# Modulation products of a hybrid transformer block on four groups of 32 array columns

## What is computed

```python
silu_c = jax.nn.silu(c)
silu_cc = jax.nn.silu(c_ctx)
mod_l = (silu_c @ w_mod[l] + b_mod[l])[:, None, :]
mod_c = silu_cc @ w_mod[l] + b_mod[l]
sh1, sc1, gt1, sh2, sc2, gt2 = jnp.split(mod_l, 6, axis=-1)
csh1, csc1, cgt1, csh2, csc2, cgt2 = jnp.split(mod_c, 6, axis=-1)
pl = modulate(rms_norm(xl, g_mix[l]), sh1, sc1) @ w_in[l]
pc = modulate(rms_norm(xc, g_mix[l]), csh1, csc1) @ w_in[l]
...
filt_l = hyena_filter(S, hy_f_w1[l], hy_f_b1[l], ...)   # sin of three small layers, then taps
...
xl = xl + gt1 * mix_l
xl = xl + gt2 * swiglu(modulate(rms_norm(xl, g_ffn[l]), sh2, sc2), w_ffn_in[l], w_ffn_out[l])
return rms_norm(xl, g_final)
```

## Time and profile before

| | us |
|---|---|
| time, median of 3 runs (lowest to highest) | 1286.63 (1286.07 to 1286.81) |
| span of the profiled execution | 1288.0 |
| TensorE busy in it | 1255.5 (97%) |
| VectorE busy | 926.2 (72%) |
| ScalarE busy | 650.4 (51%) |
| POOL busy | 305.1 (24%) |

### The profile page before, as it was taken

How to read it: one execution, slowest core, us unless ns; L and a number is a source line. 1 busy time by engine, 2 the same in 40 slices (tenths; PEclk the granted TensorE clock), 3 DMA queues, 4 the chain that set the end, 5 groups by cost and what they waited for, 6 DMA issues and landing times. The chain is left out here.

```text
span 1288.0 us, 22626 instructions
## 1 busy us (share of the span) xinstructions
PE 1255.5 (97%) x7808; PEld 658.4 (51%) x7808; DVE 926.2 (72%) x1550; ACT 650.4 (51%) x1236; POOL 305.1 (24%) x301
## 2 busy tenths in 40 slices
PE   8999999999898999999999999999999999999997
PEld 1564656544675666665455444444444444444443
DVE  3879986686688999984366976667666676566587
ACT  2532123544697999993126544444455444312424
POOL 0100000121132789960002233333322230000001
PEclk9999999999899999999999999999999999999999
DMA  9627812052240131011102222222233204998963
GB/s 359 257 95 298 294 34 66 1 164 66 67 182 1 34 131 33 0 34 66 49 33 82 68 88 66 73 75 79 90 90 90 74 32 133 319 346 270 346 219 132
DMA packets 107013, 158.89 MB, mean 123 GB/s; under 512 B 8257, under 2 KB 67137, under 8 KB 105153
## 3 DMA queue, kind: packets, MB, share of 16 engines
q1 hardware_dynamic: 106944, 158.00, 35.9%
HBM read 135.95 MB, written 19.93 MB: 121 GB/s over the span
## 5 line engine op out<-in xcount | busy, mean ns | idle before, releaser
L1116 PE MATMUL PS<-arena 128*128 128x512 f16 (+9 forms) x7208 | 1207.6, 328 | 17.1 <-DMA arena<-in_w_mod 6.2
L1116 PEld LDWEIGHTS PS<-arena 128*128 128x128 f16 (+3 forms) x7208 | 607.3, 102 | 588.1 <-issue 40.5
L2729 DVE SCALAR_TENSOR_TENSOR arena<-arena 128x512 f16<-128x512 f32 x148 | 121.0, 825 | 76.5 <-ACT arena L2026 76.5
L2026 ACT ACTIVATE arena<-arena 128x512 f16<-128x512 f32 x140 | 87.6, 629 | 130.4 <-PE PS L1116 130.4
L2633 DVE TENSOR_REDUCE arena<-PS 128x1 f32<-128x512 f32 (+1 forms) x160 | 105.7, 682 | 9.5 <-PE PS L1116 9.5
L2138 ACT ACTIVATE arena<-arena 128x512 f16<-128x512 f32 x77 | 48.1, 629 | 124.6 <-DVE arena L2880 73.8
L1962 ACT ACTIVATE arena<-PS 128x512 f16<-128x512 f32 x140 | 88.4, 632 | 2.7 <-PE PS L1116 2.2
L991 POOL TENSOR_TENSOR arena<-arena 128x2 f32<-128x2 f32 (+1 forms) x18 | 21.1, 1173 | 259.3 <-DVE arena L2485 259.3
L1031 POOL TENSOR_TENSOR arena<-arena 128x512 f16<-128x512 f32 x64 | 73.9, 1157 | 23.1 <-ACT arena L1965 21.8
L1083 POOL TENSOR_TENSOR arena<-arena 128x512 f32<-128x512 f32 x20 | 26.5, 1327 | 222.2 <-DMA arena<-in_w_ffn_in 186.5
L2657 DVE TENSOR_TENSOR arena<-PS,arena 128x512 f16<-128x512 f32 x96 | 65.5, 683 | 4.0 <-ACT PS L1965 3.9
(11 more groups left out here) (200 smaller groups left out, 1114.8 us busy)
## 6 DMA issues: line engine op xcount, KB each, us to landing
arena<-in_w_ffn_out SPq DMA_DIRECT2D x121, 256.0 KB, 5.1
arena<-in_w_mod SPq DMA_DIRECT2D x23, 1024.0 KB, 7.6
arena<-in_w_ffn_in SPq DMA_DIRECT2D x88, 256.0 KB, 3.0
arena<-in_w_in SPq DMA_DIRECT2D x9, 1024.0 KB, 5.5
left_operands<-arena SPq DMA_DIRECT2D x33, 256.0 KB, 2.2
arena<-left_operands SPq DMA_DIRECT2D x3, 2816.0 KB, 12.1
arena<-lay_bias SPq DMA_DIRECT2D x4, 1536.0 KB, 8.2
arena<-in_x SPq DMA_DIRECT2D x2, 2048.0 KB, 13.5
```

What stands on the lines that cost most here:

```text
L1116: return pe.matmul(out, lhsT, rhs, start=start, stop=stop, skip_group_check=True)
L2026: act.activation(aS[n % RING][:, 0], weight_block(p, b), ACT.Copy, scale=WS).then_inc(blk_hi, 1)
L2729: dve.scalar_tensor_tensor(dst[:, 1], src, WS, dst[:, 0], ALU.mult, ALU.subtract).then_inc(blk_lo, 1)
```

## The change

Each of the four products of a chunk writes its own 32 partitions of PSUM and so takes its own 32 columns of the array. For that the stationary operand becomes `silu_w`, the silu of c and c_ctx in columns 0 and 1 of 32, the other 30 zero (POOL clears it, ScalarE writes the two columns, and then `silu_c` as before, for the sums on VectorE). The groups turn with the chunk's number, so that over four chunks each of the four groups of each bank receives two products: the first starts its sum, the second ends it. A finished row is now in four parts, in partitions 0, 32, 64 and 96 (and 1, 33, 65, 97 for the context). ScalarE copies all 128 partitions, and the turning to columns becomes an ordinary product of `mrow` (stationary, 128 x 128) with `pick` (128 x 2), which has a one in each of the four rows that belong to a column: it turns and sums. `pick` is made on VectorE by adding up four pieces of the identity, ahead of `ident16`; TensorE waits for it before the first columns. No DMA is changed.

```diff
+        silu_w = f32(108 + 58, 8, 32)
+        pick = f32(3.25, 2)
...
             own.step(pool.memset(neghalf, -0.5))
+            own.step(pool.memset(silu_w, 0.0))
...
-                        ins = mm(PS[0:2, 2 * (c // 4) + half, :], silu_c[:, k], w[:, i, half * 512:half * 512 + 512],
-                                 k == 0, k == KD - 1)
+                        q = 32 * (2 * ((c + half) % 2) + i)
+                        ins = mm(PS[q:q + 32, 2 * (c // 4) + half, :], silu_w[:, k], w[:, i, half * 512:half * 512 + 512],
+                                 c % 4 < 2, c % 4 >= 2)
...
-                    ins = pe.transpose(PS[:, 5, o:o + 2], mrow[0:2, g, i * P:i * P + P], ident[0:2, 0:2])
+                    ins = mm(PS[:, 5, o:o + 2], mrow[:, g, i * P:i * P + P], pick, True, True)
...
             pe.wait_ge(rest_in, N_REST)
+            pe.wait_ge(id16_rdy, 1)
             modulation_columns(0)
...
-            pe.wait_ge(id16_rdy, 1)
+            pe.wait_ge(id16_rdy, 2)
...
-            act.activation(silu_c.rearrange("p k n -> p n k"),
-                           cols[:, V_C:V_C + 16].rearrange("p (n k) -> p n k", n=2), ACT.Silu).then_inc(silu_rdy, 1)
+            act.wait_ge(pool_own, 2)
+            for dst in (silu_w[:, :, 0:2], silu_c):
+                act.activation(dst.rearrange("p k n -> p n k"),
+                               cols[:, V_C:V_C + 16].rearrange("p (n k) -> p n k", n=2), ACT.Silu).then_inc(silu_rdy, 1)
...
-                act.copy(mrow[0:2, g], PSf[0:2, g * GW:g * GW + GW]).then_inc(mrow_rdy, 1)
+                act.copy(mrow[:, g], PSf[:, g * GW:g * GW + GW]).then_inc(mrow_rdy, 1)
...
+            dve.tensor_reduce(pick, ident.rearrange("p (j n) -> p n j", j=4)[:, 0:2], AX, ALU.add).then_inc(id16_rdy, 1)
             dve.tensor_copy(ident16, ident).then_inc(id16_rdy, 1)
```

## The result

| | kernel before | changed kernel |
|---|---|---|
| median | 1286.87 us (20 runs, 1285.53 to 1289.51) | 1290.68 us (20 runs, 1285.30 to 1298.38) |
| ratio | | 1.0045, 95% interval 1.0030 to 1.0059 |
| span of the profiled execution | 1288.0 us | 1286.1 us |
| mean granted TensorE clock in it | 0.995 | 0.988 |

The changed kernel is slower, by 0.45%, where 0.14% faster was forecast; the median lies just above the range. Two things have to be said of these numbers first.

What follows compares the result with a forecast made beforehand. TensorE, late on the chunks, bounded the early stage, with x's DMA landing as the wall behind it. 2.35 us won less 0.5 for the clock made -1.85: 1284.8 us, bounds 1284.3 to 1286.6, 8-in-10 range 1282.5 to 1290.0.

Steps and rivals of the forecast that it cites:

- The groups overlap: Modulation chunks on TensorE: four products on disjoint columns run at once, a chunk taking 1.0 us instead of 3.44.
- Rival 1: Modulation chunks on TensorE: groups don't overlap, chunks stay at 3.44 us, tap 2 comes 3.6 us later, 1290.2 us; chance 0.11.
- The steps up to tap 0: Stage up to VectorE's first tap: landings unchanged, then pick, mean and normalising of x; tap 0 at 36.6 instead of 40.64.
- Columns as products: Turning rows to columns on TensorE: sixteen loads take 1.8 us, +1.2 us twice; columns 0 in idle time, columns 1 paid.
- The wall at x: x's second half still lands at 41.27, so VectorE's first split starts at 44.2 instead of 46.56: 2.35 us won, no more.
- The clock: TensorE idling between 10 and 34 us brings half clock over chunks 6 and 7 and the taps; 0.5 us loss taken.
- rival 2: TensorE at half clock up to 42 us or beyond, slowing columns 1 and taps 2 to 4: 1286.5 to 1289; chance 0.18.
- What the profile after would show: List of signs in the changed profile: loads in fours, tap 0 at 36.6, x landings unchanged, half clock somewhere in 28 to 38 us.
- a lead of 2.35 us at full clock: At VectorE's first split: starts at 44.2 instead of 46.56, giving 1284.3 us if the clock stays full.
- From there the shift stays: After VectorE's first split: VectorE and TensorE busy without a gap of note, so the time won is kept.
- My base: Whole kernel: profiled span of 1288.0 us taken as 1.37 us above the median, to turn the forecast span into a time.
- rival 3: Later clock drops, around 330 and 410 us, move: 1281.4 to 1283.1 (chance 0.13) or 1286.5 to 1288.2 (chance 0.05).

Runs made afterwards that it cites:

- serial: Changed kernel with all four products on the same 32 columns, one behind the other, all else added kept; 1295.25 us, ratio 1.0071 against the kernel before.
- look3: One more profile of the changed kernel, unaltered; 1284.42 us.
- look1: One more profile of the changed kernel, unaltered; 1286.42 us.
- cols_only: Kernel before with columns 0 and 1 as ordinary products with a 2 x 2 identity in place of transposes; 1293.74 us, ratio 1.0049.

## Why the prediction was wrong

- **The groups overlap: right.** A chunk's eight loads start within 0.16 us, and at full clock chunk 4 takes 1.07 us, for my 1.0 and for the estimate of 1.1 worked out from the Trainium skill ("TensorE: Matmul & The Clock Gate", Part 3). That part's strict program order, as I read it, would have given 2.1; in the trace the first passes of chunk 4's four products start within 0.02 us and the second passes 0.45 us later, so that reading is not borne out. Rival 1 was out, and its price at tap 2 (+3.6) was met by serial (+3.66).
- **The steps up to tap 0: right.** Landings as before (x 41.6 for 41.3), `pick` at 28.4 (27.9 forecast), the mean at 32.18 (32.5), normalising at 33.56 (33.9), tap 0 at 36.80 (36.6). Columns as products cost 1.17 us each (1.2).
- **The wall at x: right, and harder than said.** With its landing between 40.5 and 43.1 in the profiles, it takes up to 1.9 us more than I gave it. I took one landing from one profile as fixed.
- **The clock: the step that failed.** I wrote that "The first unbroken work here is chunks 6 and 7 and the taps", and of rival 2 that "from chunk 7 on TensorE is busy without pause". It is, by its busy time. But columns 1 are in that stretch, and behind them the clock fell again, in three of five profiles of the changed kernel, at 39.5 to 41.7 us. I had priced columns 1 at half clock, and not as what brings the half clock; I had even noted that such products stream only two columns, and used it for columns 0 alone. In the three profiles it cost 1.5 to 3.9 us against the two without. "What the profile after would show" had one half clock somewhere in 28 to 38 us; that one came in all five, the second fall was a term that I had put at nothing.
- **Its size: mis-sized.** I took 0.5 us for the clock. For the half clock ahead of 38 us alone that was about right (0.5 to 0.9 in look3 and look1). The changed kernel's median has 41 us at half clock against 13. Much of it lies in idle time and costs nothing; but from a lead of 2.35 us at full clock the median came to +3.8, so about 6 us went to it and to what is open below. Rival 2 came nearest: taps 2 to 4 did run at half speed. But the clock did not stay down, it came back by 38.3 and fell again, and the bounds of 1286.5 to 1289 were too low.
- **"From there the shift stays": right.** It does, within the bounds given above, up to 320 us; behind that the profiles part.
- **My base was off.** I set the median 1.37 us below the span of the profiled execution and didn't see that the time lies 1.8 us above the span, so that the profiled execution was an untypical one. Falls of the clock behind 320 us (my rival 3) do move, in the kernel before too, and they are much of its spread of 4 us.
- **Open.** The upper group, above 1295 us, with 49 to 62 us at half clock, is in none of the five profiles of the changed kernel. Where its extra half clock lies is not known. That the falls behind columns 1 come with the two-column products is supported by the count over eighteen profiles, seven of eleven against none of seven. Why four of the eleven are without a fall is open. Gaps ahead of the stretch don't decide it: in cols_only TensorE was busy by the profile for 10 us and more ahead of columns 1 and the clock held, in serial it was too and the clock fell.

## What to carry to other kernels

Making TensorE faster where it then waits for DMA can cost more than it gives, because what follows runs at half clock; look for what comes right behind the faster part, see from several profiles at which clock it runs, and weigh that against the gain. A stretch of tiny products (sixteen weight loads, two columns each) is busy by the profile, and yet the clock fell behind it in seven of eleven profiles here; where no sum across groups is needed, a transpose of two rows did the same job at half the loads, with no such fall in seven. And before pricing a change of 0.2%, compare the profiled execution's own time with the median, and look at the next wait on the other engines: here the order on ScalarE had to change before any lead could stay.

## What the runs showed of the hardware

Four groups of 32 columns with 128 rows each do overlap in float32: four products of 128 x 512 take 1.07 us at full clock (1.93 at half), where one in a series of them takes 0.86. Adding 6.9 us of useless products to idle TensorE time took 0.3% off the changed kernel. And the second half of x, 2 MB behind the same bytes, landed at 40.5 to 43.1 us in the thirteen profiles that issue it at 19 to 22 us, and at 41.0 to 42.2 us in the five that issue it at 25.
